# Products of constants on TensorE in the waits of the expert routing

## What is computed

```python
x_new = x + g1 * (jnp.concatenate([ya, yb, yc, yd], axis=-1) @ w_out)     # second mixers
h2 = rms_norm_2(x_new, n2) * (1 + sc2) + sh2
x_new = x_new + g2 * expert_choice_ffn(h2, router, w_gate, w_up, w_down)

def expert_choice_ffn(h, router, w_gate, w_up, w_down):                    # 16 experts
    cap = CAPACITY_FACTOR * t // N_EXPERTS                                 # 32
    aff = jax.nn.softmax((h @ router).astype(jnp.float32), axis=-1)
    gates, idx = lax.top_k(jnp.swapaxes(aff, 1, 2), cap)
    xs = jax.vmap(lambda hb, ib: hb[ib])(h, idx)
    a = jnp.einsum('becd,edf->becf', xs, w_gate)
    u = jnp.einsum('becd,edf->becf', xs, w_up)
    y = jnp.einsum('becf,efd->becd', jax.nn.silu(a) * u, w_down)
    ...
```

## Time and profile before

| | us |
|---|---|
| median of 3 runs | 2481.4 |
| lowest and highest of them | 2475.74, 2483.57 |
| the profiled execution | 2477.95 |
| its span, first to last instruction | 2476.2 |
| PE busy | 2198.3 (89%) |
| DMA share of the chain that ended last | 17% |

### The profile page before, as it was taken

How to read it: one execution, slowest core, us unless ns; L and a number is a source line. 1 busy time by engine, 2 the same in 40 slices (tenths; PEclk the granted TensorE clock), 3 DMA queues, 4 the chain that set the end, 5 groups by cost and what they waited for, 6 DMA issues and landing times.

```text
span 2476.2 us, 33401 instructions
## 1 busy us (share of the span) xinstructions
PE 2198.3 (89%) x13670; PEld 1399.5 (57%) x13670; DVE 754.4 (30%) x1444; ACT 616.4 (25%) x905; POOL 739.8 (30%) x624
## 2 busy tenths in 40 slices
PE   8989989999799899999898999999979886787885
PEld 7866779878687798765555333333347542222221
DVE  4844221121622202365633122222146530010101
ACT  3534333434543334121521000000021410000001
POOL 7745467898183668700300000000010200000000
PEclk9989989999899899999897999999999888999998
DMA  9424759654157696431112699999982259999997
GB/s 292 137 85 153 255 181 328 234 179 170 52 171 256 217 317 222 179 118 68 51 52 119 282 428 428 429 429 428 425 305 92 96 236 423 427 427 429 429 428 296
DMA packets 151381, 635.98 MB, mean 257 GB/s; under 512 B 7816, under 2 KB 14216, under 8 KB 120920
## 3 DMA queue, kind: packets, MB, share of 16 engines
q1 hardware_dynamic: 148224, 623.78, 64.8%
q0 software_dynamic: 2608, 9.25, 1.3%
q10 hardware_dynamic: 424, 1.22, 0.2%
HBM read 633.17 MB, written 1.05 MB: 256 GB/s over the span
## 4 chain that ended last, share of the span: by engine, by line
PE 65%; DMA 17%; DVE 10%; POOL 3%; ACT 2%; issue 2%; SPq 1%; DVEq 0%; ACTq 0%
PE bank L1329 15%; DMA ring<-in_w_up 11%; PE bank L621 8%; PE bank L623 8%; PE bank L622 8%; PE bank L1169 4%; PE bank L1292 3%; PE bank L1375 3%; DMA ring<-in_w_gate 3%; DMA ring<-in_w_down 3%; POOL ring_r L1568 2%; PE bank L840 2%; PE bank L817 2%; PE bank L955 2%; PE bank L1178 2%
## 5 line engine op out<-in xcount | busy, mean ns | idle before, releaser
L1329 PE MATMUL bank<-ring,arena 128*32 128x512 f32 x4424 | 639.0, 616 | 121.4 <-DMA ring<-in_w_down 36.5
L1568 POOL TENSOR_TENSOR ring_r<-ring,ring_r 128x512 fp32r<-128x512 f32 (+1 forms) x468 | 574.9, 1268 | 315.1 <-ACT ring_r L1663 280.7
L1329 PEld LDWEIGHTS bank<-ring,arena 128*32 128x32 f32 x4424 | 192.6, 113 | 542.4 <-issue 520.1
L621 PE MATMUL bank<-ring_r 128*128 128x256 f32 (+1 forms) x1504 | 461.9, 307 | 18.2 <-DVEq L2174 9.4
L623 PE MATMUL bank<-xT_r,ring_r 128*128 128x256 f32 x1248 | 354.4, 284 | 0.0
L622 PE MATMUL bank<-ring_r 128*128 128x256 f32 x1104 | 312.6, 283 | 0.0
L621 PEld LDWEIGHTS bank<-ring_r 128*128 128x128 f32 x1504 | 288.2, 192 | 41.9 <-issue 14.0
L1663 ACT ACTIVATE ring_r<-ring 128x2048 fp32r<-128x2048 f32 (+1 forms) x119 | 216.6, 1827 | 283.4 <-DMA ring<-in_ffn_w_gu 141.5
L623 PEld LDWEIGHTS bank<-xT_r,ring_r 128*128 128x128 f32 x1248 | 239.6, 192 | 0.0
L622 PEld LDWEIGHTS bank<-ring_r 128*128 128x128 f32 x1104 | 211.5, 192 | 0.6 <-issue 0.5
L1597 POOL TENSOR_TENSOR arena<-const 128x1024 f32<-128x1024 f32 x6 | 12.1, 2022 | 656.1 <-DVEq L2174 584.1
(11 more groups left out here) (355 smaller groups left out, 2704.8 us busy)
## 6 DMA issues: line engine op xcount, KB each, us to landing
ring<-in_w_gate SPq DMA_DIRECT2D x52, 2048.0 KB, 15.9
ring<-in_w_up SPq DMA_DIRECT2D x52, 2048.0 KB, 17.2
ring<-in_w_down SPq DMA_DIRECT2D x40, 2048.0 KB, 18.1
ring<-in_ada_w SPq DMA_DIRECT2D x41, 1024.0 KB, 7.5
ring<-in_w_down SPq DMA_DIRECT2D x41, 1024.0 KB, 18.8
ring<-in_ffn_w_gu SPq DMA_DIRECT2D x35, 1024.0 KB, 5.4
ring<-in_w_up SPq DMA_DIRECT2D x18, 1024.0 KB, 8.0
ring<-in_w_gate SPq DMA_DIRECT2D x17, 1024.0 KB, 6.2
```

The lines of the kernel that those rows point to most:

```text
L621: pe.matmul(dst, w_hi, v_hi, start=first, stop=False)
L1329: mm = pe.matmul(dst[nb][CAP * b:CAP * b + CAP, :], src[:, c, CAP * b:CAP * b + CAP], rooms[b % G], start=bi_first, stop=bi_last)
L1568: pool.tensor_tensor(lo[:, c], whole[:, c], hi_of(u)[:, c, 0:n], ALU.subtract).then_inc(*signal("w_lo", (u, c)))
```

## The change

A helper `keep_busy(n)` issues `n` products of a tile of ones (`ones`, 128x128) with a constant mask (`winmask`, 128x512) into bank 7; nobody reads the result. It first waits until bank 7 has been emptied of its last real content. The helper is called at four places in layer 0 (4, 2, 1 and 4 products) and at three in layer 1 (4, 5 and 2 products); the call in `gate_slots` exists only where there are two sequences.

```diff
@@ gate_slots
                         if s < seqs - 1:
                             mm.then_inc(*signal("diag_read", layer))
+                            keep_busy(2)
@@ behind the second mixers
+                def keep_busy(n):
+
+                    pe.wait_ge(bank_free[7], filled[7])
+                    for _ in range(n):
+                        pe.matmul(bank[7][:, :], con("ones"), con("winmask"), start=True, stop=True)
@@
                 route(2 * n_half - 2)
                 route(2 * n_half - 1)
+                keep_busy(4)
                 pe.wait_ge(*after("aff", layer))
@@
                 mm.then_inc(*filled_now(("affT", layer)))
                 gate_slots()
+                keep_busy(1 if layer == 0 else 5)
                 pe.wait_ge(*after("top", layer))
@@
                 mm.then_inc(*filled_now(("posT", layer)))
+                keep_busy(4 if layer == 0 else 2)
```

## The result

| | before | changed |
|---|---|---|
| median, us | 2481.24 (6 runs) | 2469.87 (6 runs) |
| lowest and highest, us | 2475.74, 2483.57 | 2460.38, 2473.02 |
| profiled execution, us | 2477.95 | 2460.38 |
| its span, us | 2476.2 | 2458.6 |

The ratio of the changed kernel to the one before is 0.9950, with a 95% interval from 0.9929 to 0.9971: 12.4 us faster, between 7.2 and 17.6 (the two medians lie 11.4 apart). The forecast was 2468.0 with a range from 2462 to 2478, and faster by more than 0.3% as the likeliest case.

The account below looks back on a forecast made before the run. PE's low granted clock in both routings was taken to delay the weight stream; gains of 10.1 us (layer 0) and 2.5 us (layer 1), together 12.6, gave 2465.3 from the profile or 2468.8 by the median; forecast 2468, range 2462 to 2478.

Parts of the forecast that it names:

- gather: Layer 0 routing: 64 records at full clock take 7.29 us instead of 13.89, 6.6 us gained.
- first 128 expert records: First expert products of layer 0: 13.87 us at full clock instead of 16.33, 2.46 us gained.
- gain up to there, layer 0: Layer 0 through its first 128 expert records: earlier gather start, faster gather and faster expert products, 10.1 us in sum.
- gain up to there, layer 1: Layer 1: gather 3.77 instead of 6.42 us, start 0.1 us later, expert records already at full clock; 2.5 us in sum.
- DVE is late next: Layer 0, after the gate products: PE is through at 1337.2, DVE finishes `top` at 1337.74 whatever PE does.
- the four behind the positions overrun: Layer 0: four products end at 1341.6, DVE's picks come about 1340.5, so 1.1 us is given away before the gather.
- the weight stream passes the gain on: Both layers: DMA engines stand idle before the experts, so what PE gains ahead of the weight stream the stream gains too.
- Rival D: Weight stream hides PE's gain, or other executions have the gather at full clock anyway: 2477 to 2481 us; chance 0.14.
- The sign named for it: DMA picks up again about 10 us earlier in layer 0 and 2.5 us earlier in layer 1.
- The base: Starting time for the gain: profiled execution 2477.95 us gives 2465.3, the median gives 2468.8; 2468 was taken.
- Rival B: Clock falls before or among the first four products in both layers: 2470.9 to 2474.4 us; chance 0.17.
- Rival C: Products never hold the clock and each costs double, 21.8 us slower: 2499.8 to 2503 us; chance 0.07, or part of it.

Follow-up runs that it names:

- layer 0 alone: The changed kernel with the products of constants issued in layer 0 only, none in layer 1: 2472.4 us, ratio 0.9971 to the kernel before.
- the last two alone: The changed kernel with only the products behind the transposes of the positions kept, four in layer 0 and two in layer 1: 2476.3 us, one run.
- the gap filled: Changed kernel with two products behind layer 0's positions, plus two (layer 1: one) behind the first gather, while DVE scales rows: 2469.8 us, ratio 0.9948.
- one product early: Changed kernel with one of the four products ahead of the softmax moved before the last router products, both layers: 2471.8 us, ratio 0.9950.

## Why the prediction was right

By its own steps, layer 0 first, distances from R in the profile of the changed kernel:

| step | forecast | measured |
|---|---|---|
| product of constants at full clock | 0.87 us | 0.88 (3.52 for 4, from the first start to the next instruction); 0.86 between two in a row |
| start of the gather | 14.5 us | 14.4 us |
| gather | 7.29 us | 7.25 us |
| first 128 expert records | 13.87 us | 13.94 us |
| gain up to there, layer 0 | 10.1 us | 10.1 us (47.5 to 37.4) |
| gain up to there, layer 1 | 2.5 us | 2.5 us (34.5 to 31.9) |
| gain kept to the end of layer 0's experts | all | 10.1 us |

- That DVE is late next and that the four behind the positions overrun was right: DVE's picks were ready at 1337.0, the gather started at 1338.45, 1.4 us later (forecast 1.1; DVE's clearing of a tile ran beside the transposes and did not delay the picks, so they came sooner than forecast). Four products more cost their full time. Two fewer brought the gather 1.2 us forward, but in the one profile of it a fall behind the gather took that back.
- That the weight stream passes the gain on was right. Rival D had 14% and is refuted by the stretch of layer 0 in the kernel with layer 0 alone. The sign named for it came too: the DMA engines started again some 10 us sooner behind R in layer 0 and 2 to 3 us sooner in layer 1.
- The base was the uncertain part. The gain of 12.6 us from 2477.95 gives 2465.3, from the median 2468.8; measured was 2469.9, from a median of 2481.2. The choice of 2468 lay between them, and 1.9 us below the result. The 12.6 us between the lowest and the highest run are as much as the gain, so that the median came within 1.9 us of the forecast is in part luck. What bears the prediction out is the stretches above.
- Rival B exists. The early fall was seen in layer 1 in four profiles of other kernels, and in none of layer 0. Its price in layer 1, with eight behind the positions of layer 0, was 1.8 us in place of the 2.7 forecast, because the clock rose during the first four products. Its price in layer 0 was not seen. The chances name B for both layers at once; in the profiles it came in layer 1 alone, in four of thirteen. With the early fall the first 128 expert records of layer 1 ended 33.1 us behind R without products, 33.7 with all eleven, 34.1 with the last two alone and 32.9 with transposes, so the 2.5 us of layer 1 are not gained in every execution.
- Rival C never came.
- The rule of the Trainium skill (TensorE: Matmul & The Clock Gate, Part 4: PE-mode transpose) that a transpose does not count for the clock gate is not borne out in layer 0: transposes in place of all products of constants held the clock through its routing, with 1.94 us of work where the first four products had 3.68. In layer 1 of the same profile the clock fell once more, nearly 6 us after the last gate product, when PE had had only transposes and waits, so how far transposes fall short of products stays open. The gate products were there in both.

What stays open: why the fall ahead of R comes in some executions and not in others, though the instructions ahead of it are the same. The four profiles that had it were also those in which an earlier stretch of low clock, near 1920, lasted 17.1 us instead of 13.7, and in which the way from the last scatter of layer 0 to R of layer 1 took 187.8 to 188.0 us (185.8 to 187.1 in the others). So what decides it seems to act before the routing begins; what it is, no run tests. Open too is the fall in the last group, which came only in the three kernels with the gap filled or one product early, none of which has an instruction changed there. Whether the fall behind the gather follows from the shorter work ahead of it is likely and not shown.

## What to carry to other kernels

A wait of 2 to 3 us costs more than itself where the engine comes out of it at half clock into work that does not bring the clock back, and where something behind hangs on that work: here it was the start of a weight stream, and four products right ahead of the gather brought two thirds of the gain of layer 0 by themselves. Cut such filling to the length of the wait, since what overruns costs its full time; but look at the waits behind it too, since with the overrun taken away the clock fell at the end of the next one. Put some into every wait of the stretch, since one push at its start was lost again. Before reading a gain of this size, measure the executions between the same instructions: the runs of this kernel differ by as much as the change brings, in part for reasons that lie ahead of it.

## What the runs showed of the hardware that I had not expected

- Transposes can hold the granted clock (layer 0: 16 of 128 columns in 1.94 us, then 1.56 us idle, no fall until the gather had ended). In layer 1 of the same profile it fell at 2011.4, behind nearly 6 us of transposes and waits, where it did not fall with products.
- The clock can fall in or right behind a wait of 1.8 us with the gather's 64-column products ahead of it (two profiles), and it stayed full through the same wait in six others, which had more products of constants ahead of the gather. It can also fall with PE at work: 1.1 us into the gate products in one profile, and among the 16-column products of layer 1 in four.
- The 64-column gather did not bring a low clock back: it ran for 13.9 us at 0.50 without a rise, in three profiles. In the 128-column gather of layer 1 the clock rose 5.5 us after its start (2025.4 in the kernel before).
- The 64-column gather takes half as long at the full clock (7.25 against 13.89 us), although its columns alone would explain only 0.05 us of the 0.11 us a record (512 columns take 0.44). PE's weight loads are busy all the time there (PEld 2.00 of 2 us in the changed kernel's gather), and one such load takes 0.19 us at the full clock and 0.33 us at half, so the loading of weights follows the granted clock too.
